# The wide matmuls of a split-float32 expert layer read and write their two activation parts in alternating blocks of 16 columns

## The reference, cut to what matters

```python
def peer(x, w_query, sub_keys_1, sub_keys_2, expert_down, expert_up):
    ...
    def chunk(args):
        xt, et, gt = args
        u = expert_down[et]
        h = jax.nn.gelu(jnp.einsum('cd,ced->ce', xt, u), approximate=False)
        vv = expert_up[et]
        return jnp.einsum('ce,ced->cd', gt * h, vv)
```

## Time and profile before

| | before |
|---|---|
| median of 3 runs | 2432.74 us (2431.49 to 2433.75) |
| the profiled execution | 2433.66 us |
| its span, first to last instruction | 2431.4 us |
| granted TensorE clock, mean | 0.998 |
| PE busy | 2404.8 us, 99% of the span |
| DVE, ACT, POOL busy | 65%, 49%, 24% |
| matmuls | 15,884, of which 2,048 with 480 columns |

### The profile page before, as it was taken

The page is one execution under the profiler, slowest core; times in us unless marked ns, Lnnn a source line. Parts: engine busy times, 40 slices in busy tenths (PEclk is TensorE's granted clock), DMA queues, the critical chain, the costliest instruction groups (busy, mean ns, idle before and its releaser), DMA issues.

```text
span 2431.4 us, 45146 instructions
## 1 busy us (share of the span) xinstructions
PE 2404.8 (99%) x15884; PEld 2207.9 (91%) x15884; DVE 1569.1 (65%) x2615; ACT 1197.4 (49%) x1787; POOL 594.7 (24%) x427
## 2 busy tenths in 40 slices
PE   8999999999999999999999999999999999999997
PEld 8999999999999999999999999999888888888886
DVE  5555555546666666888888887755655555555556
ACT  4444444545444444666555655454444444444444
POOL 0000000000000000477668886786000000000000
PEclk9999999999999999999999999999999999999999
DMA  7667666554445665588888998988776777677764
GB/s 270 217 217 223 220 227 210 179 190 151 157 141 172 192 197 184 192 222 220 227 288 223 255 276 288 281 225 259 241 240 230 240 242 242 232 239 242 243 233 139
DMA packets 182918, 539.01 MB, mean 222 GB/s; under 512 B 53664, under 2 KB 53664, under 8 KB 180432
## 3 DMA queue, kind: packets, MB, share of 16 engines
q1 hardware_dynamic: 124128, 449.89, 56.3%
q0 software_dynamic: 54128, 71.68, 12.0%
q10 hardware_dynamic: 4608, 16.78, 2.2%
HBM read 501.42 MB, written 35.78 MB: 221 GB/s over the span
## 4 chain that ended last, share of the span: by engine, by line
PE 98%; DVE 1%; DMA 1%; ACT 0%; issue 0%; DVEq 0%; ACTq 0%; SPq 0%
PE ps L1256 38%; PE ps L1477 28%; PE ps L1452 17%; PE ps L1453 9%; PE ps L1456 1%; PE ps L1295 1%; PE ps L1310 1%; PE ps L1455 1%; PE ps L1303 0%; PE ps L1297 0%; DMA raw<-stream 0%; PE ps L1430 0%; PE ps L1311 0%; PE ps L1290 0%; DVE u_s L1209 0%; DVE u_s L1219 0%
## 5 line engine op out<-in xcount | busy, mean ns | idle before, releaser
L756 DVE TENSOR_TENSOR w_first<-raw,w_first 128x1024 fp32r<-128x1024 f32 x425 | 521.0, 1226 | 367.0 <-ACT w_first L457 355.9
L390 POOL DMA_INDIRECT g_dram<-lists x256 | 442.7, 1729 | 97.8 <-issue 79.1
L457 ACT ACTIVATE w_first<-raw 128x1024 fp32r<-128x1024 f32 x425 | 447.8, 1054 | 4.2 <-DMA raw<-stream 3.3
L756 DVE TENSOR_TENSOR w_second<-raw,w_second 128x1024 fp32r<-128x1024 f32 x299 | 365.9, 1224 | 5.4 <-ACT w_second L457 5.0
L1452 PE MATMUL ps<-a_all,w_first 128*128 128x480 f32 x1024 | 345.8, 384 | 0.2 <-DVE w_first L756 0.2
L1256 PE MATMUL ps<-a_all,w_first 128*128 128x256 f32 x2520 | 315.0, 281 | 9.2 <-DVE w_first L756 9.2
L457 ACT ACTIVATE w_second<-raw 128x1024 fp32r<-128x1024 f32 x299 | 314.6, 1052 | 7.2 <-DMA raw<-stream 6.3
L1256 PEld LDWEIGHTS ps<-a_all,w_first 128*128 128x128 f32 x2520 | 299.2, 189 | 10.2 <-issue 9.2
L1256 PE MATMUL ps<-a_all,w_second 128*128 128x256 f32 x2520 | 303.9, 276 | 0.0
L1452 PE MATMUL ps<-a_all,w_second 128*128 128x480 f32 x896 | 302.1, 382 | 0.0
L1256 PEld LDWEIGHTS ps<-a_all,w_second 128*128 128x128 f32 x2520 | 294.4, 188 | 0.0
(11 more groups left out here) (230 smaller groups left out, 3410.2 us busy)
## 6 DMA issues: line engine op xcount, KB each, us to landing
raw<-stream SPq DMA_DIRECT2D x850, 512.0 KB
g_dram<-blank POOLq DMA_DIRECT2D x32, 512.0 KB, 6.2
a_dram<-act ACTq DMA_DIRECT2D x32, 512.0 KB
a_in<-a_dram POOLq DMA_DIRECT2D x32, 512.0 KB, 5.0
g_in<-g_dram POOLq DMA_DIRECT2D x32, 512.0 KB, 6.5
g_dram<-lists POOLq DMA_INDIRECT x256
res<-x_t SPq DMA_DIRECT2D x4, 512.0 KB, 7.0
ln_s<-ln POOLq DMA_DIRECT2D x1, 2048.0 KB, 7.4
```

Source lines behind the costliest of these rows:

```text
L390: pool.indirect_dma_start(out=g_cell, out_offset=bass.IndirectOffsetOnAxis(ap=lists[0:n, tt, 1, j, c:c + 1], axis=0), in_=lists[0:n, tt, 2 ...
L457: act.activation(weights(t, hf, moved)[0], raw[:, t.slot(hf), :], ACT.Copy).then_inc(hi_ready, 1)
L756: dve.tensor_tensor(low, raw[:, s, :], high.bitcast(F32), ALU.subtract).then_inc(lo_ready, 1)
```

## The change

The low part of the activations moves from columns 240:480 of each row of `a_all` to columns 256:496, that is 1024 bytes behind the high part and no longer 960; the sum that it yields moves likewise in PSUM. The 480-column matmul no longer reads a contiguous run and no longer writes one: it takes 16 columns of the high part, 16 of the low, the next 16 of the high, and so on, 15 times each, and it writes its columns in the same order. Number, order, column counts and waits of all instructions stay as they were, and so does the 240-column matmul. The helper `turned` is defined and not called.

```diff
@@ copy_low (ACT)
-            act.activation(part[:, t.par, :], acc[t.par][:, DENSE:2 * DENSE], ACT.Copy).then_inc(part_ready, 1)
+            act.activation(part[:, t.par, :], acc[t.par][:, T:T + DENSE], ACT.Copy).then_inc(part_ready, 1)
@@ h1_low (DVE)
-            dve.scalar_tensor_tensor(out=a_all[:, k, DENSE:2 * DENSE], in0=res[:, k, 0:DENSE], scalar=small[:, S_B1 + k:S_B1 + k + 1],
+            dve.scalar_tensor_tensor(out=a_all[:, k, T:T + DENSE], in0=res[:, k, 0:DENSE], scalar=small[:, S_B1 + k:S_B1 + k + 1],
@@ down (PE)
+        def halves(v):
+
+            return v.rearrange("p (h b c) -> p b h c", h=2, c=16)[:, 0:DENSE // 16]
+
         def down(t):
...
-            both, high = acc[t.par][:, 0:2 * DENSE], acc[t.par][:, 0:DENSE]
+            both, high = halves(acc[t.par][:, 0:2 * T]), acc[t.par][:, 0:DENSE]
...
-                        pe.matmul(both, wh, a_all[:, kk, 0:2 * DENSE], start=kk == 0, stop=False)
+                        pe.matmul(both, wh, halves(a_all[:, kk, :]), start=kk == 0, stop=False)
...
-                        ins = pe.matmul(both, wh, a_all[:, kk, 0:2 * DENSE], start=False, stop=True)
+                        ins = pe.matmul(both, wh, halves(a_all[:, kk, :]), start=False, stop=True)
```

More of the change, by code:

```diff
@@ L1247, in _, with turned @@
         pe.sem_inc(half_used, HALVES_FREE)
+        def turned(v, n):
+            return v.rearrange("p (a b c) -> p b a c", a=n, c=16)
         def half_ready(t, hf):
```

## The result

The changed kernel takes 2450.05 us (median of 4 runs, 2449.61 to 2455.12) against 2432.32 us for the kernel before (4 runs too), a ratio of 1.0077, 95% interval 1.0060 to 1.0094: **17.7 us slower**, where 25 us faster was forecast. The profiled execution is the longest of the four, 2455.12 us with a span of 2452.8.

What follows compares the result with a forecast made beforehand. PE was taken to bound the kernel: 26.8 us gained in 480-column matmuls less 1.5 us of new waits gives -25.3 from 2433.66, 2408.4; the profiled execution being 0.9 above the median, 2407.5 us. Range 2396 to 2438.

Steps and rivals of the forecast that it cites:

- What bounds the kernel; where the change acts.: PE, busy 99% of the span, sets the time; the change acts on 2048 480-column matmuls, mostly in the down stage.
- The moves of the low part and its sum: 0.: `h1_low` and `copy_low` access the same 240 columns at another offset, shape unchanged: 0.
- If meetings of the two streams make the excess, this changes it.: 480-column matmuls: meetings of moving and weight reads may make the 20 ns excess; the new order would change it.
- Taking the middle, 13.1 ns gained.: 480-column matmuls: excess falls from 20 to 6.9 ns, as in undisturbed 256-column runs; 26.8 us gained over 2048.
- Rival 2, slower by the joins.: 480-column matmuls: 29 joins at one cycle, 0.42 ns, each cost 25 us in all, 2458 us; chance 0.22.
- The sign for costly joins: Profile of the changed kernel: 480-column duration rises above 383 ns by 12 ns or more, nothing else changes.
- The rule against the change.: Skill text on PSUM: any non-contiguous access pattern slows matmuls significantly, so the 480-column matmul becomes slower; no figure.
- What a faster PE runs into: 1.5 us.: New PE waits for the weight stream from 1231 to 1252 us and in later fetches: 1.5 us lost.
- the full gain: 480-column matmuls: the whole 20 ns excess goes, 41 us; POOL would then hold the up stage up by some 4 us.
- The range.: Whole kernel: 2396 us, upper gain less POOL's part, to 2438, covering no change; slower cases left out.

Runs made afterwards that it cites:

- e1: Changed kernel, but the wide matmul reads and writes 240 high columns, then 240 low ones 1024 bytes behind; 2433.63 us.
- e4: Changed kernel with `a_all` and the two buffers behind it (`res`, `cst`) 64 bytes further on; 2484.72 us.
- e13: Changed kernel, but 14 of 16 pairs per tile in the down stage load 32 weight columns, not 128; 2437.89 us.
- e14: Kernel before the change, but 14 of 16 pairs per tile in the down stage load 32 weight columns, not 128; 2419.14 us.
- e3: Kernel with the wide matmul reading 480 contiguous columns as before the change, but writing by turns of 16; 2436.71 us.
- e5: Changed kernel with turns of 8 columns instead of 16, 59 joins instead of 29; 2448.68 us.
- e9: Kernel with one contiguous run as before the change, but taking every second block of 16, then the blocks between; 2440.28 us.
- e2: Changed kernel, reading by turns of 16 but writing 480 contiguous columns; 2449.88 us.
- e8: Changed kernel, turns of 16 kept, with the low part again 960 bytes behind the high one; 2450.38 us.
- e12: Kernel before the change, with weight loads in the down stage taking every second column of a run of 256; 2448.63 us.

## Why the prediction was wrong, step by step

- *What bounds the kernel; where the change acts.* Right. What moved is the pace of the pairs in the down stage; the up stage and the long 256- and 258-column runs kept theirs.
- *The moves of the low part and its sum: 0.* Right: e1, 679.5 us.
- *"Reading 16 from one run and 16 from another makes the moving operand go through its addresses at half its former pace ... If meetings of the two streams make the excess, this changes it."* **This step failed.** It rested on rows in which the excess depends on layout, which is true and e4 shows it again, and went on to one partner for the moving reads, the weight loads, and from there to a gain. The excess did change with the order of addresses, but upward, and not by meetings with the weight loads: with loads of a quarter of the columns the turned order still costs 10.9 ns a pair (e13 against e14). The reads of the moving operand have a cost of their own in this order, 8.8 ns a matmul.
- *Taking the middle, 13.1 ns gained.* The sign of that term was open, since no row had a broken order, and I took it from the runs of other shapes. Measured: each pair became 8.8 ns longer; 18.0 us lost in PE's pace where 26.8 were to be gained.
- *Rival 2, slower by the joins.* Right in sign and near in size (25 us by one cycle a join; 18.0 measured, 0.30 ns a join where 0.42 was assumed), and wrong about where. It named both operands, PSUM with its jump of 1024 bytes. PSUM has no part in it (e3), and joins have no fixed price (e5, e9), so that the size came near was luck.
- *The sign for costly joins: the 480-column record 12 ns or more above 383, nothing else changed.* It would have missed this case: that record grew by 6 ns, and those of the unchanged narrow matmul and of the loads by 5 to 6 too.
- *The rule against the change.* "PSUM — Partial Sum Buffer" in the Trainium skill, Specifications, has any non-contiguous pattern slow matmuls. e3 with blocks of 16 shows no such cost. The sentence of "Advanced Engine Details and Errata" in the Trainium skill, Memory Cachelines, that every two consecutive elements should be contiguous, agrees with e3. The kernel became slower as the first rule says, for another reason.
- *What a faster PE runs into: 1.5 us.* Not tried by the change, since PE was not faster. In e14 the stage was 14.1 us shorter and the time 13 us shorter, so others took back little of that. PE waited 1.8 us for the stream there; but it waited 1.1 us in the slower changed kernel too, so this doesn't bear the 1.5 us out. What POOL does at the full gain no run reached.
- *The range.* It ended at 2438 and left the slower cases out, 22% by my own count. The price of this one stood in the text, from 25 to 50 us, and the measured one lies below both.

**What stays open:** why reading at half pace in small blocks costs. The runs say what it is not (writing, place against the weights, distance, number of joins) and, within the limits of e13 and e14, that it is not the weight loads. They don't say what it is. Nor that half pace is the right name for it: blocks of 48 and 80 go at half pace on the whole too and cost 2.1 and 1.8 ns. That blocks of 120 are faster than a contiguous run, by 1.7 ns a pair in both executions, is measured and not explained.

## What to carry to other kernels

Where a change only reorders what an operand reads, and the trace has no such order, the sign is open: measure it in a small variant before building on it, or let both signs into the range. Reading and writing can be split in two small variants like e2 and e3, and the suspected partner made smaller as in e13 and e14, always in both orders, since only the difference of differences tells. And when matmuls are back to back, compare the pace over many tiles in a stretch without waits; single records shift, and the length of a stage carries waits of 0 to 2 us that differ from one execution to the next, as large as some effects here.

## What the runs showed of the hardware that was not expected

- The place of the activations matters by bytes: 32 or 64 bytes further on, 256-column matmuls took 118.5 ns on average (102.42 us / 864) and not 113.6, the loss being in those that read `a_all` (records of 283 ns and not 276); 256 bytes back nothing changed. The whole kernel lost 32 to 35 us by that (2481.94 and 2484.72, one execution each, against 2450.05): in e4, 7.4 us in the up stage, and 22.7 before the down stage, which began at 1059.0 us and not 1036.3.
- A float32 matmul of 480 columns whose moving operand is read in blocks of 16 out of order is 3.8 to 9.2 ns slower, by the order (3.8 in e9, 9.2 in e8); in blocks of 48, 2.1. Writes to PSUM in blocks of 16 cost nothing (e3: 330.1 ns a pair against 330.8).
- Weight columns at step 2 lengthen a load of 128 from 188 to 190 ns to 193 to 198, and a stage of 2048 pairs by 12.4 us (e12).
- Matmuls of 480 and 240 columns with 32 weight columns and not 128, in 14 of 16 pairs, have a pace of 322.9 ns a pair and not 330.8 (e14), though by the records the loads of 188 ns overlap the matmuls.
